# GpSimd instead of VectorE subtracts the rounded gated values from the gated values, between its row gathers

## The reference, cut to what matters

```python
def block_fn(args):
    xb, eb, gb = args
    a = jax.nn.gelu(jnp.einsum('tkd,td->tk', u_table[eb], xb), approximate=False)
    return jnp.einsum('tk,tkd->td', gb * a, v_table[eb])
```

## Time and profile before

| what | us |
|---|---|
| median of 3 runs | 1432.2 |
| profiled execution, first to last instruction (span) | 1431.5 |
| TensorE busy | 1390.2 (97%) |
| VectorE busy | 1207.8 (84%) |
| GpSimd busy | 782.1 (55%) |
| ScalarE busy | 708.0 (49%) |

### The profile page before, as it was taken

One profiled execution on the slowest core, in us unless ns is written; L12 is line 12 of the kernel. 1 busy time (PEld: TensorE's weight loads), 2 busy tenths in 40 slices (PEclk: granted clock), 3 DMA queues, 4 the chain that ended last, 5 costly groups with the idle time before them and its releaser, 6 DMA issues.

```text
span 1431.5 us, 23514 instructions
## 1 busy us (share of the span) xinstructions
PE 1390.2 (97%) x8449; PEld 1277.6 (89%) x8449; DVE 1207.8 (84%) x2633; ACT 708.0 (49%) x1315; POOL 782.1 (55%) x466
## 2 busy tenths in 40 slices
PE   6998899999999999999999999999999999999999
PEld 2464566878999999999999999899999999999999
DVE  5756887764989899988998876589999999999997
ACT  1244775233344886478835863344433334433442
POOL 0001000301578877878877778848755648577560
PEclk9899799999999999999999999999999999999999
DMA  9830011354679999999999999999999999999996
GB/s 353 309 113 1 1 60 59 118 191 171 237 255 312 357 329 350 409 386 338 324 399 390 326 343 385 413 348 398 401 390 388 393 398 386 401 399 401 400 401 228
DMA packets 158229, 438.81 MB, mean 307 GB/s; under 512 B 16608, under 2 KB 50720, under 8 KB 156832
## 3 DMA queue, kind: packets, MB, share of 16 engines
q1 hardware_dynamic: 91632, 244.55, 46.8%
q0 software_dynamic: 46080, 167.79, 30.3%
q10 hardware_dynamic: 20400, 24.95, 4.9%
HBM read 390.02 MB, written 47.22 MB: 305 GB/s over the span
## 4 chain that ended last, share of the span: by engine, by line
PE 87%; DMA 3%; DVE 3%; POOL 3%; ACT 2%; issue 1%; SPq 1%; ACTq 0%; DVEq 0%
PE ps L1292 11%; PE ps L1293 11%; PE ps L1291 11%; PE ps L1240 10%; PE ps L1242 10%; PE ps L1241 10%; PE ps L1251 5%; PE ps L985 5%; PE ps L1111 2%; POOL lo L577 2%; PE ps L1082 1%; DMA qkc<-in_w_ada 1%; PE ps L1153 1%; PE ps L1139 1%; PE ps L1150 1%; PE ps L1141 1%
## 5 line engine op out<-in xcount | busy, mean ns | idle before, releaser
L835 ACT ACTIVATE hi<-raw 128x1024 fp32r<-128x1024 f32 x256 | 270.8, 1058 | 214.7 <-DMA raw<-in_v_tiles 148.3
L577 POOL TENSOR_TENSOR lo<-raw,hi 128x1024 fp32r<-128x1024 f32 x123 | 296.3, 2412 | 146.7 <-ACT hi L835 137.3
L1240 PE MATMUL ps<-h2hi,hi 128*128 128x352 f32 x1024 | 336.3, 328 | 5.3 <-POOL lo L577 5.3
L1242 PE MATMUL ps<-h2hi,lo 128*128 128x352 f32 x1024 | 331.5, 324 | 0.0
L1241 PE MATMUL ps<-h2lo,hi 128*128 128x352 f32 x1024 | 331.0, 323 | 0.0
L1292 PE MATMUL ps<-clo,hi 128*128 128x352 f32 x1008 | 324.1, 322 | 0.0
L1293 PE MATMUL ps<-chi,lo 128*128 128x352 f32 x1008 | 324.1, 322 | 0.0
L1291 PE MATMUL ps<-chi,hi 128*128 128x352 f32 x1008 | 324.1, 322 | 0.0
L590 POOL DMA_INDIRECT row_res<-in_v_tiles,E x91 | 175.3, 1926 | 99.5 <-DVE y_tok L1768 65.2
L1240 PEld LDWEIGHTS ps<-h2hi,hi 128*128 128x128 f32 x1024 | 193.8, 189 | 7.5 <-POOL lo L577 7.4
L1241 PEld LDWEIGHTS ps<-h2lo,hi 128*128 128x128 f32 x1024 | 193.5, 189 | 0.0
(11 more groups left out here) (300 smaller groups left out, 2185.2 us busy)
## 6 DMA issues: line engine op xcount, KB each, us to landing
raw<-in_u_tiles SPq DMA_DIRECT2D x128, 512.0 KB
raw<-in_v_tiles SPq DMA_DIRECT2D x128, 512.0 KB
gelus<-act_out ACTq DMA_DIRECT2D x128, 176.0 KB
act_in<-gelus SPq DMA_DIRECT2D x128, 176.0 KB
gates<-stage SPq DMA_DIRECT2D x32, 512.0 KB
gate<-gates SPq DMA_DIRECT2D x32, 512.0 KB
late<-in_w_ada SPq DMA_DIRECT2D x4, 2048.0 KB, 8.1
qkT<-in_w_ada SPq DMA_DIRECT2D x3, 2048.0 KB, 20.5
```

The lines of the kernel that those rows point to most:

```text
L577: nc.gpsimd.tensor_tensor(lo[m % 3][:], raw[m % 3][:], hi[m % 3][:].bitcast(F32), ALU.subtract).then_inc(u_lo, 1)
L835: nc.scalar.activation(hi[m % 3][:], raw[m % 3][:], ACT.Copy).then_inc(t_hi, 1)
L1240: nc.tensor.matmul(out, hi[n % 3][:, cols], dense(h2hi, k), start=(k == 0), stop=False)
L1242: last = nc.tensor.matmul(out, lo[n % 3][:, cols], dense(h2hi, k), start=False, stop=(k == KD - 1))
```

## The change

The function `low_c` moves from VectorE's list to GpSimd's, with the same operands and the same semaphore. On GpSimd it additionally waits for `y_ps`, for the buffer of `clo` that it writes. The first three subtractions stand ahead of the gathers of the second half; then, for each n, GpSimd issues the gathers whose row was freed by the row sums of steps before n, and then subtracts for tile n+3.

```diff
--- before.py
+++ after.py
@@ -598,6 +598,21 @@
+
+            def low_c(n):
+                pool.wait_ge(c_hi, n + 1)
+                if n >= 4:
+                    pool.wait_ge(y_ps, n - 3)
+                nc.gpsimd.tensor_tensor(clo[n % 4][:], cf[n % 2][:], chi[n % 4][:].bitcast(F32), ALU.subtract).then_inc(c_lo, 1)
+
+            for n in range(3):
+                low_c(n)
+            for n in range(NT):
+                while g < 2 * SU and row_step[g - NROWS] < NT + n:
+                    gather(g)
+                    g += 1
+                if n + 3 < NT:
+                    low_c(n + 3)
             while g < 2 * SU:
                 gather(g)
                 g += 1
@@ -1745,10 +1760,6 @@
-            def low_c(n):
-                dve.wait_ge(c_hi, n + 1)
-                tt_(clo[n % 4][:], cf[n % 2][:], chi[n % 4][:].bitcast(F32), ALU.subtract).then_inc(c_lo, 1)
-
@@ -1783,11 +1794,8 @@
             low_v(0)
-            low_c(0)
             weigh(2)
             low_v(1)
-            low_c(1)
-            low_c(2)
             for n in range(NT):
@@ -1796,8 +1804,6 @@
-                if n + 3 < NT:
-                    low_c(n + 3)
```

## The result

| | kernel before | changed kernel |
|---|---|---|
| time, median of 4 runs each (us) | 1431.43 (1429.41 to 1434.67) | 1458.54 (1455.41 to 1459.71) |
| span of the profiled execution (us) | 1431.5 | 1457.1 |
| first matmul of the products with v to the last fused pair (us) | 936.5 to 1417.8 = 481.3 | 932.9 to 1443.3 = 510.4 |

The ratio is 1.0178, 95% interval 1.016 to 1.0196: the change costs 27.1 us, or 1.8%. The forecast was 1444 us, 12 us over the kernel before, so sign and mechanism came out as worked out there, and the loss is more than twice the size. The profiled span differs by 25.6 us only, less than the 29.1 us of the second half, because in this execution the second half happened to begin 3.6 us earlier.

A forecast was written before the change was run, and what follows sets the result against it. TensorE bounds the products with v at 3.82 us a tile; VectorE's mean step rises from 3.69 to 3.92. 124 x 0.10 - 3.7 = 8.7 us, plus 3 for waits for v and 0.7 to the median, gives 1444 us; range 1430 to 1465.

The forecast's parts named there:

- the price of a double step: Steps with two row sums: subtraction falls between the sums, +0.48 less 0.44 us, so 4.68 becomes 4.72 us.
- the lead: Start of the products with v: VectorE is ahead, so 3.7 us are used up before TensorE waits.
- The bound: Products with v: TensorE full at 3.82 us a tile; VectorE at 3.69 us a step has 0.13 us to spare.
- The mechanism: GpSimd's subtraction and VectorE instructions with two SBUF operands do not run together; one stands until the other is over.
- The price of a single step: Steps with one row sum: 0.75 us added to VectorE, less 0.44 removed, so 3.28 becomes 3.59 us.
- 4.00 us a step: VectorE's mean step if double steps pay in full: 0.18 us over TensorE's, costing 18.6 us.
- That just suffices: GpSimd's queue: gather takes the low part's end, subtraction the row sum's end, with 0.25 us of margin; no cost.
- rival B: GpSimd's queue places don't suffice, every gather and subtraction costs VectorE a handover: 4.18 us a step, 1473 us; chance 0.10.
- VectorE's remaining waits for v: VectorE's waits for tiles of v may not vanish altogether; put at 3 us.
- A: Rival: not slower, the subtraction finds VectorE idle and TensorE stays full, 1432 us; chance 0.30, of which 0.03 a gain.
- C: Rival: first come first served, subtraction let in behind whatever runs, 4.00 us a step, 1451 us; chance 0.18.

The follow-up runs named there:

- VectorE twice: Kernel before, with VectorE's own subtraction done twice from the fifth tile on, the first time into unused memory: 1467.24 us, ratio 1.0221.
- the run with one operand: Changed kernel with every row sum but two replaced by a reduction that takes one operand from SBUF: 1433.51 us, ratio 0.9994.
- its control: Kernel before with the same replacement of row sums by one-operand reductions, the subtraction staying on VectorE: 1431.61 us, ratio 0.9986.
- doubles-only kernel: Changed kernel with GpSimd subtracting only for the 36 tiles in steps with two row sums, VectorE for the other 92: 1434.56 us, ratio 0.9995.
- low-part-first kernel: Changed kernel with GpSimd's subtraction issued ahead of the gathers in each step instead of behind them: 1450.01 us, ratio 1.0101.
- late: Changed kernel with a 128-column fill on GpSimd ahead of each subtraction from the fifth tile on: 1458.71 us, ratio 1.0159.
- the singles: Changed kernel, GpSimd doing 92 subtractions, VectorE the 36 in double steps: 1463.64 us behind the gathers, 1441.33 us ahead of them.

## Why the prediction was right, and where it was wrong

The forecast was +12 us, the measurement +27. What failed are three terms of the sum: the price of a double step, a queue whose misses were put at nothing, and the lead.

**The bound: right.** TensorE was full before and VectorE had 0.13 us a step to spare; nothing was gained by relief of VectorE, and its excess went into the time (VectorE twice: +0.29 a step gave 35 us).

**The mechanism: right.** That GpSimd's subtraction and VectorE's instructions with two operands from SBUF exclude each other was inferred from three meetings elsewhere in the trace; the run with one operand and its control show it for this place. The price of a single step, +0.75 - 0.44, came out at 3.59 us. That it fits to the hundredth is in part luck: with the subtraction ahead of the gathers most single steps take 3.53.

**"In a double step the subtraction can fall between the two row sums ... 4.68 becomes 4.72": the step that failed first.** It can, and did in 8 of the 34 double steps in which no sum is opened; in the other 26 it was let in ahead of the first sum, and the step was 4.95 us. What was mis-sized is +0.48, which measured 4.95 - 4.68 + 0.44 = 0.71 there: 26 x 0.23 = 6 us. The forecast had this end in its working (4.00 us a step) and chose the lower one on a possibility, not on a row. In the doubles-only kernel 20 of 34 fell between the sums, so the price hangs on where the queue happens to stand.

**"That just suffices": the second.** The 0.25 us of margin was right as arithmetic, since the subtraction did begin 0.36 us before the row sum's end, but it didn't secure the place: 12 were passed over all the same, at 0.60 us, 7 us in all. This was rival B's mechanism in a tenth of the steps, and at another price than B's. The low-part-first kernel, with no misses, stands at a ratio of 1.0101 instead of 1.0178, and "late", with 12 and timed beside it, at 1.0159: 9 us between those two, of which some 3 are its single steps of 3.53 (52 x 0.06).

**"3.7 us are used up before TensorE waits": the third.** TensorE lost 29.1 us and VectorE's chain 123 x 0.241 = 29.6. At the end the distance from the last row sum to the fused pair shrank from 7.0 to 5.6 us, which gave 1.4 back, and at the start the first row sum came 5.0 us after TensorE's first matmul in place of 4.1, which took 0.9. A net 0.5 us, not 3.7.

The terms again with their measured sizes: 12.4 us (124 x 0.10) + 6 for the doubles + 7 for the misses + VectorE's remaining waits for v, 5.5 instead of 3, make 31 against the 29.6 measured, less 0.5 for the lead. The 1.3 us between them is not traced.

**Rivals.** A (hidden, 1432) fell: the handover was paid in every step. C (first come first served, 4.00 a step, 1451) came nearer than the forecast, for a reason that the trace refutes: the subtraction of 983.59 was not let in behind the instruction then running. The Trainium skill (SBUF — State Buffer, Who interferes with whom) has the same contention, VectorE with two SBUF inputs against GpSimd's reads, and on that part this trace agrees, with 1.97 against 1.28 us in the row sum and 1.21 in the reduction with one input. By the recorded starts its rule that the order of issue decides who blocks isn't borne out in the 12 misses, nor in the L1761 of 987.73: this had been running for 0.58 us when GpSimd's subtraction began by the profile at 988.31, and it still ended only 0.13 us after that one.

## What to carry to other kernels

Work moved from VectorE to GpSimd is not moved beside VectorE when both read two operands from SBUF: here each 128x352 subtraction of 0.44 us of VectorE's time became 0.71 to 0.75 us of its standing still, and 0.48 where it fell between two row sums; so look first whether VectorE's instructions there have one operand in PSUM or only one at all. If such work must go to GpSimd, issue it ahead of the gathers rather than behind them (1450 against 1459 us, and 1441 against 1464 for the singles), and only so often that VectorE's mean step stays about at the bound (36 or 64 of the 128 cost nothing that shows). And where an engine is 97% busy, read how far each step is from the bound in hundredths of a microsecond: the 0.24 us a step here were 29 us, and a digit in the page's slices does not show it.

## What the runs showed of the hardware that was not expected

- A GpSimd subtraction that waits beside VectorE's unbroken chain can be passed over: with a lead of 0.34 to 0.38 us on the row sum's end, 35 were let in there and 12 only at the low part's end, and those took 2.80 instead of about 1.26 us. In both kernels with the subtraction ahead of the gathers none was passed over, though 35 and 34 of them came with the same lead of 0.36 to 0.37 us, for reasons that stay open.
- The instruction that pays need not be the one that was running when GpSimd's began: the 96-column multiplication took 1.67 us instead of 0.25 though GpSimd's subtraction began, by the profile, 0.58 us after it. With a fill of 0.22 us ahead of the subtraction it was the low part of v, which began 0.57 us ahead of the subtraction and took 2.62 us instead of 1.22. What holds them in that half microsecond stays open; a gather is running then in both.
- A wait of TensorE costs a little more than the idle time that the profile gives it. In the timeline of TensorE, these are the last matmul before a gap and three behind it:

```profile
1106.71 0.32 PE L1308 MATMUL ps<-chi,lo 128*128 128x352 f32 x1
1107.66 0.43 PE L1306 MATMUL ps<-chi,hi 128*128 128x352 f32 x1 [0.62 <-DVE lo L1766]
1107.92 0.33 PE L1307 MATMUL ps<-clo,hi 128*128 128x352 f32 x1
...
1111.48 0.32 PE L1308 MATMUL ps<-chi,lo 128*128 128x352 f32 x1
```

The pitch of the matmuls is 0.159 us, so the one of 1107.66 was due at 1106.87 and is 0.79 us late, of which the row calls 0.62 idle; the next comes 0.26 us behind it, another 0.10; and from 1107.92 to 1111.48 the pitch of 22 matmuls is 0.162, which adds another 0.07. It is in part why the 16.1 us of idle time in L1306's group fall short of the 29.1 us lost.
